# Key-cache pages loaded from POOL's queue, between the value pages, instead of from SP's

## What is computed

```
layer 0: x += W_o . attention_A(rope(qknorm(W_qkv . rmsnorm(x))))     # 16 heads of 64, one block of 256, causal
         x += W_down . (silu(g) * u),  [g u] = W_gu . rmsnorm(x)      # dense, 2816 wide
shared keys and values for layer 1 from x                             # 8 heads
layer 1: x += W_o . merge of three dilated windows(q_0, q_1, q_2)     # 3 groups x 8 heads
         x += top-2-of-8 experts of rmsnorm(x)                        # 3584 wide
samples: keys and values of 256 past positions come from caches,
         for layer 0 from pages of 128 positions by page_table
outputs: x, and the new keys and values of both mixers
```

## Time and profile before

| what | value |
|---|---|
| median of 3 runs | 1756.66 us (1755.32 to 1757.08) |
| the profiled execution: its time, its span | 1757.08 us, 1755.4 us |
| PE busy | 1651.1 us, 94% |
| DVE busy | 1339.1 us, 76% |
| ACT busy | 1030.9 us, 59% |
| POOL busy | 50.1 us, 3% |
| DMA | 453.49 MB, mean 258 GB/s |
| key pages of A: DMAs, us to landing (median) | 32, 4.7 |
| value pages of A: DMAs, us to landing (median) | 32, 3.9 |

### The profile page before, as it was taken

One profiled execution on the slowest core, in us unless ns is written; L12 is line 12 of the kernel. 1 busy time (PEld: TensorE's weight loads), 2 busy tenths in 40 slices (PEclk: granted clock), 3 DMA queues, 4 the chain that ended last, 5 costly groups with the idle time before them and its releaser, 6 DMA issues.

```text
span 1755.4 us, 25120 instructions
## 1 busy us (share of the span) xinstructions
PE 1651.1 (94%) x9238; PEld 1369.3 (78%) x9238; DVE 1339.1 (76%) x1540; ACT 1030.9 (59%) x995; POOL 50.1 (3%) x73
## 2 busy tenths in 40 slices
PE   6999989999998785699999999999999999999998
PEld 6885589999887555578888888878878878878886
DVE  5775366655677645898898888888888988988987
ACT  5434344443443323477777777777777777777775
POOL 0002110000000102000000000000000000000000
PEclk9999899999999787799999999999999999999999
DMA  9348325535630530499999999999999999999995
GB/s 331 116 139 269 115 96 171 169 114 150 224 124 21 178 138 13 168 335 341 355 342 344 353 346 341 353 333 355 350 332 359 344 338 358 343 332 363 338 341 199
DMA packets 236693, 453.49 MB, mean 258 GB/s; under 512 B 8224, under 2 KB 80032, under 8 KB 236368
## 3 DMA queue, kind: packets, MB, share of 16 engines
q1 hardware_dynamic: 231568, 434.40, 70.9%
q0 software_dynamic: 5056, 18.16, 3.1%
HBM read 447.81 MB, written 4.72 MB: 258 GB/s over the span
## 4 chain that ended last, share of the span: by engine, by line
PE 87%; DVE 6%; ACT 3%; DMA 1%; issue 1%; DVEq 0%; SPq 0%; ACTq 0%
PE psum L277 24%; PE psum L279 24%; PE psum L278 24%; PE psum L781 1%; PE psum L816 1%; PE psum L796 1%; PE psum L591 1%; PE psum L580 1%; DVE wlo L273 1%; PE psum L567 1%; DVE rs L1185 1%; ACT whi L269 1%; PE psum L632 1%; PE psum L566 1%; PE psum L521 1%
## 5 line engine op out<-in xcount | busy, mean ns | idle before, releaser
L273 DVE TENSOR_TENSOR wlo<-raw,whi 128x2048 fp32r<-128x2048 f32 (+1 forms) x404 | 911.8, 2262 | 207.9 <-ACT whi L269 207.5
L269 ACT ACTIVATE whi<-raw 128x2048 fp32r<-128x2048 f32 (+1 forms) x404 | 764.6, 1895 | 303.8 <-PE psum L279 303.7
L277 PE MATMUL psum<-whi,xgh 128*128 128x512 f32 x896 | 360.2, 402 | 10.0 <-DVE wlo L273 8.6
L278 PE MATMUL psum<-wlo,xgh 128*128 128x512 f32 x896 | 355.4, 397 | 0.0
L279 PE MATMUL psum<-whi,xgl 128*128 128x512 f32 x896 | 355.3, 397 | 0.0
L277 PE MATMUL psum<-hh,whi 128*128 128x288 f32 x800 | 246.5, 308 | 14.2 <-DVE hl L1318 8.5
L279 PE MATMUL psum<-hh,wlo 128*128 128x288 f32 x800 | 240.7, 301 | 0.0
L278 PE MATMUL psum<-hl,whi 128*128 128x288 f32 x800 | 240.0, 300 | 0.0
L277 PEld LDWEIGHTS psum<-whi,xgh 128*128 128x128 f32 x896 | 169.1, 189 | 52.2 <-DVE wlo L273 12.2
L279 PEld LDWEIGHTS psum<-whi,xgl 128*128 128x128 f32 x896 | 169.1, 189 | 40.9
L278 PEld LDWEIGHTS psum<-wlo,xgh 128*128 128x128 f32 x896 | 169.3, 189 | 38.3
(11 more groups left out here) (297 smaller groups left out, 1612.8 us busy)
## 6 DMA issues: line engine op xcount, KB each, us to landing
raw<-in_w_gu_moe SPq DMA_DIRECT2D x226, 1024.0 KB, 5.2
raw<-in_w_down_moe SPq DMA_DIRECT2D x112, 1024.0 KB, 5.0
raw<-in_w_gu_dense SPq DMA_DIRECT2D x22, 1024.0 KB, 5.1
raw<-in_w_qkv_a SPq DMA_DIRECT2D x12, 1024.0 KB, 11.3
raw<-in_w_down_dense SPq DMA_DIRECT2D x16, 704.0 KB, 4.6
kraw_a<-in_cache_a_k SPq DMA_DIRECT2D x32, 256.0 KB, 4.7
vraw_a<-in_cache_a_v POOLq DMA_DIRECT2D x32, 256.0 KB, 3.9
raw<-in_w_q_b SPq DMA_DIRECT2D x6, 1024.0 KB, 5.1
```

What stands on the lines that cost most here:

```text
L269: nc.scalar.activation(whi[:, p % SPL, 0:size], raw[:, p % RAW, 0:size], ACT.Copy).then_inc(hi_ready, 1)
L273: nc.vector.tensor_tensor(wlo[:, p % SPL, 0:size], raw[:, p % RAW, 0:size], whi[:, p % SPL, 0:size].bitcast(F32), ALU.subtract).then_inc(p ...
L277: nc.tensor.matmul(out, lh, rh, start=start, stop=False)
L278: nc.tensor.matmul(out, lh, rl, start=False, stop=False)
```

## The change

The function `key_page` moves with all key pages to POOL: SP's list loses all key pages, and POOL's new function `caches` issues them together with the value pages, by a table that says behind which key page each value page stands.

```
-KEYS_AT = 20
+VALUES_A = [9] * 4 + [16, 16, 18, 18] + [24, 24, 26, 26] + [32] * 4
+VALUES_B = [7] * 3 + [16] * 5
...
         @block.sync
...
-            eng.wait_ge(sem("pages_loaded"), 16)
-            for n in range(A["kring"]):
-                key_page(eng, A, n)
-            for p in range(RAW, KEYS_AT):
-                load_piece(eng, 0, p, W[p])
-            for n in range(A["kring"], 4 * A["nj"]):
-                key_page(eng, A, n)
-            for p in range(KEYS_AT, PRE):
+            for p in range(RAW, PRE):
                 load_piece(eng, 0, p, W[p])
...
-            eng.wait_ge(sem("ktok_done_b"), B["nj"])
-            eng.wait_ge(sem("vtok_done_b"), B["nj"])
-            for n in range(4 * B["nj"]):
-                key_page(eng, B, n)
...
         @block.gpsimd
...
-            def values_loaded(b):
-
-                eng.wait_ge(sem(f"kv_stored_{b['tag']}"), 64)
-                for n in range(2 * b["nj"]):
-                    value_pages(b, n)
-
+            def caches(b, first):
+
+                v = 0
+                for n in range(first, 4 * b["nj"]):
+                    key_page(b, n)
+                    if n == first + 3:
+                        eng.wait_ge(sem(f"kv_stored_{b['tag']}"), 64)
+                    while v < 2 * b["nj"] and b["vafter"][v] == n:
+                        value_pages(b, v)
+                        v += 1
+                while v < 2 * b["nj"]:
+                    value_pages(b, v)
+                    v += 1
+
+            for n in range(A["kring"]):
+                key_page(A, n)
             store(A, io["ak"], io["av"])
-            values_loaded(A)
+            caches(A, A["kring"])
...
             eng.wait_ge(sem("vtok_done_b"), B["nj"])
+            for n in range(B["kring"]):
+                key_page(B, n)
             store(B, io["bk"], io["bv"])
-            values_loaded(B)
+            caches(B, B["kring"])
```

More of the change, by code:

```diff
@@ L161, in build_program @@
         A["score_banks"], A["pt_bank"], A["pv_bank"], A["kt_banks"], A["s_bank"] = ((0,), (1,), (7,)), 2, 3, (4, 5), 6
+        A["vafter"], B["vafter"] = VALUES_A, VALUES_B
         B["score_banks"], B["pt_bank"], B["pv_bank"], B["kt_banks"], B["s_bank"] = ((0, 1, 2),), 3, 4, (5, 7), 6
@@ L315, in gain @@
             return cst[:, a + k:a + k + 1]
[L318 to L330, removed]
         @block.sync
@@ L405, in store, with key_page @@
                     eng.dma_start(out[SEQ:T, :], buf[0:NSAMP, 2, :]).then_inc(sem(f"kv_stored_{b['tag']}"), 16)
+            def key_page(b, n):
+                tg, slot = b["tag"], n % b["kring"]
+                z, q, page = n // 8, 4 * (n // (2 * b["nj"])) + n // 2 % 4, n % 2
+                if n >= b["kring"]:
+                    eng.wait_ge(sem(f"ktr_done_{tg}"), n - b["kring"] + 1)
+                if b is A:
+                    pg = eng.value_load(pgt[0:1, 2 * q + page:2 * q + page + 1], min_val=0, max_val=NPHYS - 1)
+                    src = io["cache_a_k"][0][bass.ds(pg, 1), :, 512 * (z % 2):512 * (z % 2) + 512].rearrange("a p n -> p (a n)")
+                else:
+                    src = io["cache_b_k"][q][P * page:P * page + P, :]
+                eng.dma_start(b["kraw"][:, slot, :], src).then_inc(sem(f"kraw_loaded_{tg}{slot}"), 16)
             def value_pages(b, n):
```

## The result

| | before | after |
|---|---|---|
| median of 4 runs | 1756.84 us (1755.32 to 1757.08) | 1783.43 us (1779.15 to 1789.33) |
| profiled execution: time, span | 1757.08, 1755.4 us | 1783.73, 1782.0 us |
| PE's mean granted clock | 0.966 | 0.952 |

The change makes the kernel slower: ratio 1.0154, interval [1.0133, 1.0175]. The forecast was 1779, and its range from 1766 to 1792 holds the measured median.

The account below looks back on a forecast made before the run. PE (TensorE), busy 94% of the span, was taken as the bound. 1757.1 + 18.2 (stalls 5.0 + 15.0, less 1.8 swallowed) + 5.1 clock - 1.3 mixer B = 1779.1, given as 1779, range 1766 to 1792.

Parts of the forecast that it names:

- The pitch: POOL's queue in mixer A's attention: each key or value page takes 1.15 us to issue, 2.07 while the stores run.
- stall 1: Mixer A's attention: PE waits for key page 10 behind eight value DMAs, 4.6 us, plus 0.4 for page 11; 5.0 us.
- Stalls 2 to 5: Mixer A's attention: key pages 17, 19, 25, 27 each late behind four value DMAs; 3.9, 3.8, 3.5, 3.8, sum 15.0 us.
- Pages 6 and 7: Mixer A's key pages behind 2.3 MB of stores in one queue: cost 0, between -1.5 and +1.5 us.
- the waits for scaling: Mixer A's attention: two of PE's four waits for ACT's scaling, directly behind pages 19 and 27, go; -1.8 us.
- The clock: Mixer A: PE's clock falls behind pages 11, 19 and 27, 1.7 us each; 5.1 us in all.
- rival 2: Landings stretch to 6.3 us beside DVE, or POOL's register reads stay at 2 us per page: 1792.5 us, chance 0.10.
- The start: A's first six key pages on POOL share DMA engines with the first weights: hidden, 0, at worst +1 us.
- Mixer B: B's attention: first key pages go ahead of the stores, first softmax ends sooner; -1.3 us, from -2.5 to +2.
- SP and the rest: SP's queue without key pages gains nothing: its next weight piece waits for a buffer; the expert stage keeps its length.

Follow-up runs that it names:

- fillers: Changed kernel with 16 dummy matmuls ahead of PE's waits for key pages 10, 17, 19, 25 and 27 of mixer A; 1772.93 us, 1.0080 of the kernel before.
- a_only: Changed kernel with mixer B's key pages back on SP and its value pages directly behind the stores; 1783.41 us, 1.0142 of the kernel before.
- b_only: Kernel before with only mixer B's key pages moved to POOL, in the changed kernel's order; 1758.99 us, ratio 1.0000.
- first_only: Changed kernel with A's value pages 0 to 3 left ahead of key page 10, 4 to 15 moved behind key pages 21 to 32; 1761.56 us, ratio 1.0017.
- keys_first: Changed kernel with A's key pages 6 to 9 ahead of the stores and its value pages behind key pages 15 to 31; 1757.51 us, 0.9988 of before.
- before_busy: Kernel before, key pages still on SP, with 27 dummy matmuls on PE in both attention stages; 1739.39 us, ratio 0.9891.
- static_pages: Changed kernel with A's cache pages read at fixed places, without register reads from the page table; 1774.73 us, 1.0097 of the kernel before.
- late_values: Changed kernel with A's value pages behind key pages 15, 21, 23, 29 and 31, all key pages still on POOL; 1760.09 us, 1.0011 of before.
- kept_busy: Changed kernel with A's key pages 6 to 9 ahead of the stores, value pages late, and 27 dummy matmuls in both mixers; 1742.94 us, 0.9912 of before.

## Why the prediction was right, and where its steps were not

- **The pitch and stall 1: right.** First value DMA 139.48 (139.9 predicted), the eighth 147.43 (147.95), page 10 issued 148.58 (149.1). Pages 6 to 9 went out (137.69 - 131.49)/3 = 2.07 us apart, as on SP. The last store landed 8.0 us after its issue at 130.30, at 138.3 (138.2). The wait was 3.7 us, not 4.6: the issue came 0.5 us sooner and landings were 3.3 us (median), not 3.6.
- **Stalls 2 to 5: the places right, two sizes too large.** Page 17 went out 4.60 us after value page 4, as counted, and waited 3.44 us (3.9), page 25 3.32 (3.5). Pages 19 and 27 waited 1.10 and 2.31 us where 3.8 stood for each. The step that failed is the count of when PE wants them: it assumed PE's work between the two turns at full clock, 165.44 - 163.05 = 2.4 us. At 1.2 GHz it took 177.16 - 172.42 = 4.7 us, so PE was late itself. Five waits, 13.9 us, instead of 20.0.
- **Pages 6 and 7, and the waits for scaling: right.** One wait of 2.44 us stands where 1.50 and 0.89 stood. Of PE's four waits for ACT's scaling two are left, -1.8 us.
- **The clock: the mechanism right, the size wrong.** 5.1 us were put down, 11.8 were paid. The sum took one short spell of before (3.4 us, 1.7 lost) for each of three stalls. The spells in and behind them were 6.8, 17.1 and 13.7 us; the two at the end of the stage, of 10.2 and 6.8, answer to those of 13.7 and 6.8 before. `fillers` had no spell from 143 to 232 us, and 13.2 us came back. In part the two errors are one: where POOL limits, slow work fills the wait. The slow work between the turns of 17 and 19 took 2.35 us more and that between 25 and 27 1.6 more; counted as waits, as the sum did, they make the five stalls 17.9 us instead of 20.0 and leave 7.9 for the clock instead of 5.1. Stalls and clock together were 23.3 in the sum and 23.9 in the trace, and this near agreement is partly luck.
- **POOL's DMAs beside DVE: rival 2 did not occur.** The value pages' and the key pages' DMA groups of the changed kernel (ns min/median/max; rows 5 of before), and the landings of the value pages:

```profile
L407 POOL DMA_DIRECT2D vraw_a<-in_cache_a_v x32: 538/538/538, 139.5 to 227.0; - x32
...
DMA to landing us min/median/max: 2.8/3.3/5.0
```

```profile
L395 POOL DMA_DIRECT2D kraw_a<-in_cache_a_k x32: 538/538/708, 9.1 to 207.3; - x32
```

  The starving that the Trainium skill (SBUF — State Buffer, section "SBUF: two separate sides") describes for POOL's queue beside DVE doesn't show in these rows; they don't tell whether DVE ran such a copy beside them. The longest landing of a value page was 5.0 us, not 6.3, and the five late key pages landed in 3.3 to 3.6 us. Pages 6 to 8, issued while the stores ran, took 7.4, 5.9 and 4.4.
- **The start: right.** First split 15.17 (15.01), first weight matmul 19.44 (19.29 before), first rotation 30.66 (30.51); the scores of A start 0.1 us later.
- **Mixer B: the term is not borne out.** The row that answers to rows 11 shows page 0 as the late one, with 1.24 us:

```profile
597.55 1.97 PE L593 MATMUL psum<-cst,kraw_b 128*128 128x128 f32 x8 [1.24 <-DMA kraw_b<-in_cache_b_k]
```

  Until 660.9 us B had gained 1.05 us (lag 23.70 to 22.65), near the -1.3 predicted. But `a_only`, with B's pages on SP, gained as much up to the same matmul (20.88 to 19.86), so the move itself won next to nothing. Then B lost 1.8 us up to the next wait for a softmax and 1.5 more up to its output projection, in spells of 17.1 and 6.8 us where before had 6.8 and 3.4. The term had no clock in it. As `a_only` shows the same stage length, this is not the move's own price. Between the two profiled executions the sum lacks 4.7 us (22.0 against 26.65), and 3.5 of it stand here.
- **SP and the rest:** nothing gained, as predicted. SP issues four expert pieces before 590 us that stood behind B's key pages, to no effect; from B's output projection to the end it is 0.7 us more.

## What to carry over

A page that the bottleneck engine needs soon must not stand in one queue behind pages that it needs later, above all behind ones that wait for that same engine; which queue it is mattered little. Issuing the pages faster is no cure by itself: here the landings grew as the pitch fell. When TensorE waits, count what follows at the lower clock too: here 12.1 us of waits cost 11.8 more. Where a stage waits often in small pieces, try matmuls without use ahead of the waits before you rearrange transfers.

## What the runs showed of the hardware that was not expected

- The clock can fall behind a short wait and stay low while PE works without a pause. The spell of before from 201 to 215 us lies in a window with PE busy for 14.00 of 14 us. The last wait ahead of it, for ACT's scaling, was of 1.16 us and ended 0.6 us before:

```profile
200.47 0.65 PE L644 MATMUL psum<-cst,pvs_a 128*64 128x16 f32 x16 [1.16 <-ACT pvs_a L979]
```

  `b_only`, with the same work in A, has the spell too. `first_only`, `fillers` and `keys_first` have the same wait at the same place of the work and no spell behind it; `before_busy`, with a matmul in that wait, has one spell of 6.8 us in all of A. The Trainium skill (TensorE: Matmul & The Clock Gate, section "HAM oscillation — how this bites in real kernels") describes a clock that falls over waits for DMAs. The changed kernel's spells at 149 and 170 agree with it (0.52 and 0.50; they begin 1.1 and 1.9 us into waits of 3.7 and 3.4 us); the spell at 201 before the change had no wait for a DMA near it. What decides such a spell stays open.
- A gain ahead of such spells need not last: `keys_first` was 4.5 us ahead at the end of A in its trace, and its ratio is 0.9988 [0.9972, 1.0005]. Its A had 10.2 us at 1.2 GHz, its B three spells of 17 to 20 us.
- A register read of the page table is slow on POOL too while the stores run, as on SP. The four reads from 129 to 139 us, and all 32 (ns min/median/max):

```profile
L391 POOLq TENSOR_LOAD <-pgt x4: 860/948/1284, 129.7 to 135.8; - x4
```

```profile
L391 POOLq TENSOR_LOAD <-pgt x32: 284/291/1284, 7.6 to 206.1; - x32
```

  Without these reads (`static_pages`) the same four pages went out within 2.2 us, from 130.39 on, but page 6 was turned at 138.94 as in the changed kernel (138.91): its landing grew instead. What in the stores slows the reads was not tried.
- One kernel's time varies with its granted clock. first_only ran from 1754.04 us (0.968) to 1766.09 (0.958), late_values from 1752.37 (0.969) to 1766.39 (0.961). The kernels with matmuls in the waits of both stages varied least, before_busy from 1738.29 to 1740.53 and kept_busy from 1742.19 to 1745.49, but they have only four and five runs.
